# Request cross-attention in a decoder step: 32-column score groups, and values with the probabilities as stationary operand

## The reference, cut to what matters

```
def _cross_attn(h, mk, mv, w_cq, w_co):
    b, s, _ = h.shape
    q = (h @ w_cq).reshape(b, s, MEM_HEADS, MEM_HEAD_DIM)
    sc = jnp.einsum('bshd,bmhd->bhsm', q, mk).astype(jnp.float32) * (MEM_HEAD_DIM ** -0.5)
    p = jax.nn.softmax(sc, axis=-1).astype(mv.dtype)
    o = jnp.einsum('bhsm,bmhd->bshd', p, mv).reshape(b, s, MEM_WIDTH)
    return o @ w_co
```

## Time and profile before

| | |
|---|---|
| median of three runs | 2350.18 us |
| the profiled execution | 2351.52 us |
| its span in the trace | 2349.7 us |
| TensorE busy with products | 2241.3 us, 95% |
| VectorE busy | 1185.6 us, 50% |
| ScalarE busy | 300.5 us, 13% |
| moved by DMA | 843.21 MB, mean 359 GB/s |
| the changed stage, scores of v = 4 to the start of the output projection | 846.4 to 912.2 us |

### The profile page before, as it was taken

The page is one execution under the profiler, slowest core; times in us unless marked ns, Lnnn a source line. Parts: engine busy times, 40 slices in busy tenths (PEclk is TensorE's granted clock), DMA queues, the critical chain, the costliest instruction groups (busy, mean ns, idle before and its releaser), DMA issues.

```text
span 2349.7 us, 35545 instructions
## 1 busy us (share of the span) xinstructions
PE 2241.3 (95%) x14334; PEld 2050.4 (87%) x14334; DVE 1185.6 (50%) x2106; ACT 300.5 (13%) x923; POOL 370.0 (16%) x414
## 2 busy tenths in 40 slices
PE   7999998788889899999999999999999999999996
PEld 5677776576589889999999999999999999999996
DVE  3100004834376734867777644288644444444445
ACT  2000002612130001111111110144100000000001
POOL 0100000013201111222222221012211111111110
PEclk9999999999999988999999999999999999999998
DMA  7999962289859995899999999788999999999996
GB/s 290 399 410 390 395 259 80 105 345 372 327 202 403 373 346 216 338 395 421 422 421 421 418 422 420 289 307 339 367 422 422 422 422 422 422 422 421 421 422 247
DMA packets 117787, 843.21 MB, mean 359 GB/s; under 512 B 14432, under 2 KB 16608, under 8 KB 30656
## 3 DMA queue, kind: packets, MB, share of 16 engines
q1 hardware_dynamic: 62752, 485.30, 51.5%
q0 software_dynamic: 54128, 354.58, 37.3%
q10 hardware_dynamic: 816, 2.11, 0.2%
HBM read 834.25 MB, written 74.78 MB: 387 GB/s over the span
## 4 chain that ended last, share of the span: by engine, by line
PE 64%; DMA 26%; DVE 7%; ACT 1%; issue 1%; SPq 0%; POOL 0%; DVEq 0%; POOLq 0%; ACTq 0%
PE low L1383 50%; DMA BIG<-expert_v,VB 23%; PE big L1383 13%; DVE XT L1227 3%; DMA WR<-wall 1%; ACT BIG L607 1%; DMA BIG<-kaT 1%; DMA BIG<-memT 0%; DVE CST L939 0%; DVE BIG L816 0%; PE low L1513 0%; PE low L1559 0%; PE big L1733 0%; DVE CST L998 0%; DVE XT L1378 0%
## 5 line engine op out<-in xcount | busy, mean ns | idle before, releaser
L1383 PE MATMUL low<-HT,WR 128*128 128x176 f32 (+3 forms) x6336 | 1085.4, 334 | 7.3 <-DMA WR<-wall 6.0
L1383 PEld LDWEIGHTS low<-HT,WR 128*128 128x128 f32 x6336 | 989.8, 192 | 95.4 <-issue 7.7
L1227 DVE SCALAR_TENSOR_TENSOR XT<-BIG,VB,XT 128x2048 f32<-128x2048 f32 x128 | 301.0, 2352 | 333.5 <-DMA BIG<-expert_v,VB 333.2
L1383 PE MATMUL big<-BIG,WR 128*128 (+3 forms) x2888 | 451.0, 312 | 14.9 <-DVE XT L862 7.1
L1383 PEld LDWEIGHTS big<-BIG,WR 128*128 128x128 f32 x2888 | 417.6, 193 | 36.7 <-issue 24.6
L1383 PE MATMUL low<-BIG,WR 128*128 (+3 forms) x2616 | 434.5, 321 | 10.5 <-DMA WR<-wall 10.5
L1383 PEld LDWEIGHTS low<-BIG,WR 128*128 128x128 f32 x2616 | 411.5, 192 | 15.0 <-issue 10.6
L1214 DVE SCALAR_TENSOR_TENSOR BIG<-BIG 128x2048 f32<-128x2048 f32 x144 | 329.7, 2291 | 177.4 <-DMA BIG<-expert_u,VB 176.1
L519 POOL DMA_INDIRECT BIG<-expert_u,VB x144 | 164.2, 1140 | 763.1 <-DVE BIG L1214 683.5
L525 POOL DMA_INDIRECT BIG<-expert_v,VB x144 | 142.8, 991 | 591.8 <-DVE XT L1227 497.2
L885 DVE TENSOR_SCALAR BIG<-low 128x320 f32 x32 | 15.8, 492 | 264.0 <-PE low L1383 264.0
(11 more groups left out here) (226 smaller groups left out, 1107.4 us busy)
## 6 DMA issues: line engine op xcount, KB each, us to landing
WR<-uT SPq DMA_DIRECT2D x128, 1024.0 KB, 10.1
WR<-expert_v SPq DMA_DIRECT2D x128, 1024.0 KB, 14.5
WR<-wall SPq DMA_DIRECT2D x122, 1024.0 KB, 8.9
BIG<-va POOLq DMA_DIRECT2D x48, 512.0 KB, 8.7
BIG<-kaT POOLq DMA_DIRECT2D x64, 384.0 KB, 12.5
BIG<-kmT SPq DMA_DIRECT2D x2, 2048.0 KB, 10.2
BIG<-vm SPq DMA_DIRECT2D x8, 512.0 KB, 11.7
XT<-xT SPq DMA_DIRECT2D x1, 2560.0 KB, 21.6
```

Source lines behind the costliest of these rows:

```text
L1227: nc.vector.scalar_tensor_tensor(out=x_tok, in0=rows_of(row), scalar=weight, in1=x_tok, op0=ALU.mult, op1=ALU.add).then_inc(s_vsum, 1)
L1383: return nc.tensor.matmul(out, lhsT, rhs, start=start, stop=stop, skip_group_check=True)
```

## The change

The scores of a request group become 16 products with 32 columns each. The query block is laid out by request, and each head of it sits at its own 8 of 32 columns (`qpad_c` shrinks from 2176 to 512 words); request n writes only partitions 32n to 32n+32 of the bank, and the four heads add up there. The order is heads outside, requests inside, so that four products in a row use four different column groups. In the values, the probabilities of a request, transposed, are the stationary operand (32 columns), and all 512 value columns (4 heads x 128) the moving one: 8 products for a group, again four column groups in a row. That gives each row the values of all four heads. ScalarE copies the bank to `o_req`, and four more products with `own_head` (the identity with the rows of the other heads set to zero) turn it and pick each row's own head. VectorE prepares `is_head` and `own_head` ahead. The second request group moves from v = 9 to v = 8, and the last prompt head from v = 8 to v = 9. VectorE reorders group 0 in step 4 of the pipeline and group 1 at its end. The second group's values are now loaded when the four-column values of the first are done (`s_cV`), at the same place of the queue.

```
+        qpad_c = BIG[:, 11264:11776].rearrange("p (n h c) -> p n h c", n=4, h=4)
+        own_head = BIG[:, 11776:12288].rearrange("p (h c) -> p h c", h=4)
+        o_req = BIG[:, 12288:12800]
+        V_FIRST, V_REQ, V_ALL = 0, (4, 8), 10
+        HEAD_OF = {0: 0, 1: 1, 2: 2, 3: 3, 5: 0, 6: 1, 7: 2, 9: 3}
+        KEPT = {v: i + 1 for i, v in enumerate((0, 1, 2, 3, 5, 4, 6, 7, 9, 8))}
...
                 if before == POS["pq", 0, 12]:
-                    sp.wait_ge(s_cO, V_REQ[0] + 1)
+                    sp.wait_ge(s_cV, 1)
                     mem_values(1)
...  (ScalarE, in step it)
+                if 4 + it - 2 in V_REQ:
+                    r = V_REQ.index(4 + it - 2)
+                    act.wait_ge(s_cV, r + 1)
+                    nc.scalar.activation(o_req, bank[5], ACT.Copy).then_inc(s_cVev, 1)
...  (VectorE)
-            def out_requests():
-                dve.wait_ge(s_cO, V_ALL)
-                for r in range(2):
+            def out_requests(r):
+                dve.wait_ge(s_cO, KEPT[V_REQ[r]])
...
-                    nc.vector.memset(qpad_c, 0.0)
+                    nc.vector.memset(BIG[:, 11264:11776], 0.0)
+                    for h in range(4):
+                        nc.vector.tensor_scalar(own_head[:, h, :], ident, is_head[:, h:h + 1], None, ALU.mult)
...
-                if 4 <= it <= 7:
+                if 4 <= it <= 6:
                     out_c(v - 3)
+                if it == 4:
+                    out_requests(0)
                 if it < 7:
                     next_row()
-            out_requests()
+            out_c(9)
+            out_requests(1)
...  (TensorE, scores)
-                    for m in range(16):
-                        ins = mm(o, qpad_c[:, m * P:(m + 1) * P], km[:, m * MEM:(m + 1) * MEM], start=(m == 0), stop=(m == 15))
+                    for h in range(4):
+                        for n in range(4):
+                            ins = mm(o[32 * n:32 * n + 32, :], qpad_c[:, n, h, :], km[:, (4 * n + h) * MEM:(4 * n + h + 1) * MEM], start=(h == 0), stop=(h == 3))
...  (TensorE, values)
-                    for n in range(4):
-                        for h in range(4):
-                            m = 4 * n + h
-                            for b in range(2):
-                                ins = mm(bank[5][:, r * P + m * 8:r * P + m * 8 + 8], vm[n][:, b * 512 + h * P:][:, 0:P], pT[:, b * P + m * 8:b * P + m * 8 + 8], start=(b == 0), stop=(b == 1))
+                    if r:
+                        pe.wait_ge(s_cOev, KEPT[V_REQ[0]])
+                    for b in range(2):
+                        for n in range(4):
+                            ins = mm(bank[5][32 * n:32 * n + 32, :], pT[:, b * P + 32 * n:b * P + 32 * n + 32], vm[n][:, b * 512:(b + 1) * 512], start=(b == 0), stop=(b == 1))
+                    ins.then_inc(s_cV, 1)
...
+            def own_values_c(r):
+
+                pe.wait_ge(s_cVev, r + 1)
+                for h in range(4):
+                    ins = mm(bank[5][:, 0:P], o_req[:, h * P:(h + 1) * P], own_head[:, h, :], start=(h == 0), stop=(h == 3))
                 ins.then_inc(s_cO, 1)
...  (TensorE, in step it, behind the values)
+                if 4 + it - 3 in V_REQ:
+                    own_values_c(V_REQ.index(4 + it - 3))
```

More of the change, by code:

```diff
@@ L233, in build @@
         probsT_c = [BIG[:, at:at + 512].rearrange("p (b c) -> p b c", b=2) for at in (16000, 10240)]
-        qpad_c = BIG[:, 11264:13440]
+        qpad_c = BIG[:, 11264:11776].rearrange("p (n h c) -> p n h c", n=4, h=4)
+        own_head = BIG[:, 11776:12288].rearrange("p (h c) -> p h c", h=4)
+        o_req = BIG[:, 12288:12800]
+        is_head = stat[:, 76:80]
         km = BIG[:, 0:4096]
@@ L340, in build @@
         s_cpad = sem("c_pads")
+        s_cV, s_cVev = sem("c_request_values"), sem("c_request_values_kept")
         s_xt, s_ht = sem("tile0_turned"), sem("tile0_rows")
@@ L641, in turned_c @@
                 act.wait_ge(s_cT, v + 1)
-                if v >= 2:
-                    act.wait_ge(s_cO, v - 1)
+                if v - 2 in V_REQ:
+                    act.wait_ge(s_cV, V_REQ.index(v - 2) + 1)
+                elif v >= 2:
+                    act.wait_ge(s_cO, KEPT[v - 2])
                 nc.scalar.activation(probsT_of(v), turn_out(v), ACT.Copy).then_inc(s_cTev, 1)
@@ L1049, in pads_c @@
                 for h in range(4):
-                    dst = qpad_c.rearrange("p (n h c) -> p n h c", n=4, h=4)[:, :, h, 0:QPR]
+                    dst = qpad_c[:, :, h, QPR * h:QPR * (h + 1)]
                     src = qc[1][:, h, P + 32 * r:P + 32 * r + 32].rearrange("p (n q) -> p n q", q=QPR)
@@ L1068, in out_c @@
             def out_c(v):
-                dve.wait_ge(s_cO, v + 1)
-                dst = oc[0][:, v, :] if v < V_REQ[0] else oc[1][:, v - V_REST, 0:P]
+                dve.wait_ge(s_cO, KEPT[v])
+                dst = oc[0][:, v, :] if v < V_REQ[0] else oc[1][:, HEAD_OF[v], 0:P]
                 nc.vector.tensor_copy(dst, values_out(v)).then_inc(s_cOev, 1)
-            def out_requests():
-                dve.wait_ge(s_cO, V_ALL)
-                for r in range(2):
-                    for h in range(4):
-                        src = bank[5][:, r * P:(r + 1) * P].rearrange("p (n h q) -> p n h q", n=4, h=4)[:, :, h, :]
-                        dst = oc[1][:, h, P + 32 * r:P + 32 * r + 32].rearrange("p (n q) -> p n q", q=QPR)
-                        ins = nc.vector.tensor_copy(dst, src)
-                    ins.then_inc(s_cOev, 1)
+            def out_requests(r):
+                dve.wait_ge(s_cO, KEPT[V_REQ[r]])
+                for h in range(4):
+                    src = bank[5][:, 0:P].rearrange("p (n h q) -> p n h q", n=4, h=4)[:, :, h, :]
+                    dst = oc[1][:, h, P + 32 * r:P + 32 * r + 32].rearrange("p (n q) -> p n q", q=QPR)
+                    ins = nc.vector.tensor_copy(dst, src)
+                ins.then_inc(s_cOev, 1)
+            nc.vector.tensor_copy(is_head, head_mask.rearrange("p (h e) -> p h e", h=4)[:, :, 0])
             softmax_s(0)
@@ L1635, in scores_c @@
                 if V_FIRST + 2 <= v < V_REQ[0]:
-                    pe.wait_ge(s_cOev, v - 1)
+                    pe.wait_ge(s_cOev, KEPT[v - 2])
                 elif v >= V_REQ[0] + 2:
@@ L1643, in scores_c @@
                     pe.wait_ge(s_cpad, 4 * r + 4)
-                    for m in range(16):
-                        ins = mm(o, qpad_c[:, m * P:(m + 1) * P], km[:, m * MEM:(m + 1) * MEM], start=(m == 0), stop=(m == 15))
+                    for h in range(4):
+                        for n in range(4):
+                            ins = mm(o[32 * n:32 * n + 32, :], qpad_c[:, n, h, :], km[:, (4 * n + h) * MEM:(4 * n + h + 1) * MEM], start=(h == 0), stop=(h == 3))
                     ins.then_inc(s_cS, 1)
                 else:
-                    q = qc[0][:, v, :] if v < V_REQ[0] else qc[1][:, v - V_REST, 0:P]
-                    h = v if v < V_REQ[0] else v - V_REST
+                    h = HEAD_OF[v]
+                    q = qc[0][:, h, :] if v < V_REQ[0] else qc[1][:, h, 0:P]
                     mm(o, q, km_p[:, h * MEM:(h + 1) * MEM]).then_inc(s_cS, 1)
@@ L1665, in values_c @@
                     pe.wait_ge(s_vm[r], 4 * 16)
-                    for n in range(4):
-                        for h in range(4):
-                            m = 4 * n + h
-                            for b in range(2):
-                                ins = mm(bank[5][:, r * P + m * 8:r * P + m * 8 + 8], vm[n][:, b * 512 + h * P:][:, 0:P], pT[:, b * P + m * 8:b * P + m * 8 + 8], start=(b == 0), stop=(b == 1))
-                else:
-                    if v >= V_REST + 2:
-                        pe.wait_ge(s_cOev, v - 2)
-                    h = v if v < V_REQ[0] else v - V_REST
+                    if r:
[4 more added lines that the diff above has]
+                    ins.then_inc(s_cV, 1)
+                else:
+                    if v in (7, 9):
+                        pe.wait_ge(s_cOev, KEPT[5 if v == 7 else 7])
+                    h = HEAD_OF[v]
                     for b in range(2):
                         ins = mm(values_out(v), vm_p[:, b * 512 + h * P:b * 512 + (h + 1) * P], pT[:, b * P:(b + 1) * P], start=(b == 0), stop=(b == 1))
+                    ins.then_inc(s_cO, 1)
+            def own_values_c(r):
+                pe.wait_ge(s_cVev, r + 1)
+                for h in range(4):
+                    ins = mm(bank[5][:, 0:P], o_req[:, h * P:(h + 1) * P], own_head[:, h, :], start=(h == 0), stop=(h == 3))
                 ins.then_inc(s_cO, 1)
```

1 line of the change is left out of this document (removed).

## The result

| | before | after |
|---|---|---|
| median (four runs each, same chips) | 2349.59 us | **2325.97 us** |
| lowest to highest | 2346.76 to 2351.24 | 2323.5 to 2330.9 |
| profiled execution, its span | 2351.52, 2349.7 | 2326.72, 2324.9 |
| scores of v = 4 to start of the output projection | 65.8 us | 45.8 us |

The ratio after to before is 0.9907 with a 95% interval of 0.9892 to 0.9922: the kernel is about 0.9% faster. The forecast was 2324.2 us.

What follows compares the result with a forecast made beforehand. TensorE was taken to bound the changed stage, with DMA room: 32.1 us of work + 1.8 + 4.9 + 2.7 + 2.7 = 44.2 against 70.15 us, 26 us less, so 2324.2 us from median 2350.2; range 2316 to 2335.

Steps and rivals of the forecast that it cites:

- Scores in column groups: Request scores in the changed stage: 32 records at 58 ns, 1.85 us per group, 3.7 us for both.
- lost clock: At the stage's first scores, behind 3.10 us of TensorE idle time: 1.8 us lost, expected to stay.
- Values of the first group: Request values in the changed stage: 16 records of 512 moving columns, 1.85 us per group.
- Half clock at the end: Values of v = 8, picking and the four products behind run half at 1.2 GHz: 2.7 us more.
- Waits: TensorE's waits in the changed stage: 4.9 us for VectorE's steps plus 2.7 us for the second group's values.
- the late load: Second group's values before v = 8: landing at 880 us, wanted at 877.3, 2.7 us beyond 1.5 us already counted.
- Column groups that don't run side by side: Rival, 2%: no parallel column groups in the stage's scores and values, 20.6 us less gain, 2341 us.
- The DMA queue in TensorE's place: Rival, 9%: late values and gathers in the stage make TensorE wait; gain 10 to 16 us, 2334 to 2340 us.
- the wait for `vm`: Sign at the second group's values: the forecast is wrong if TensorE's wait for their load exceeds 5 us.
- the slower case: Rival, 3%: clock stays at 1.2 GHz behind the sparse steps into the output projection and beyond; up to 2360 us.
- given back: Rival, 3%: the stage's transfers pile up before the full DMA engines from 1036 us on; the end stays at 2350.
- Edits at nothing: Small edits counted as free: memset 1.87 to some 0.4 us, four scalings of 0.28 us, ScalarE's copy of 0.60 us.

Runs made afterwards that it cites:

- the change again: The changed kernel itself, unaltered, run on another chip beside later runs; median 2325.47 us, ratio 0.9898 to the kernel before.
- values loaded first: Changed kernel with the second group's values loaded ahead of the output projection's first two weight chunks; median 2318.53 us, ratio 0.9876 to the kernel before.
- values alone: Changed kernel with the request scores computed as before the change, values and picking kept; median 2329.56 us, ratio 0.9926 to the kernel before.
- other order: Changed kernel with the loop over requests outside, so products in a row use the same column group; median 2325.24 us, ratio 0.9901 to the kernel before.
- five rows later: Changed kernel with values loaded before two weight chunks, first query block laid out earlier, five expert rows moved out of the pipeline; 2317.29 us, 0.9864 to before.

## Why the prediction was right, point by point

**The bound.** Right: what TensorE lost in this stage came out at the end. From the start of the output projection to the end of the span it is 1437.5 us before and 1433.8 after; of the 3.7 us, 1.8 are the half clock in the first records of the earlier trace rows, now gone, and 1.7 a wait of TensorE for VectorE in the last stages, 7.4 us instead of 9.1. Nine further traces of changed kernels have 1434.0 to 1434.7 us here, whatever their stage gained; the change again has 1436.7, and only the two that move most rows out of the stage have more. Over the 70.15 us counted in the prediction the kernel now takes 48.44 us, 21.7 less; the stage began 1.2 us earlier (0.6 of it is there at 690 us already, 0.6 arises at a wait for a DMA near 760 us), and with the 1.7 us behind it these are 24.6 of the 24.8 us of the spans.

**Luck.** The stage gave 21.7 us and not the 26 forecast. Another 2.9 us (1.2 ahead of it, 1.7 behind) are from places that the change hardly touches and that differ from execution to execution: the stage starts between 842.98 and 847.81 us in traces whose instructions ahead of it are nearly the same, and the last wait is 5.6 us in the change again. That the total came within 2 us of the forecast is in part chance.

**The sum.** 48.44 us against 44.2 forecast. By terms, from start to start in the rows:
- Scores in column groups: 1.87 us for the second group, 1.85 forecast; the ideal, 8 x 0.221, is 1.77 us, so the two changes of mode around it cost 0.1 us at most. The first took 2.61 of the 3.65 forecast, and the tile behind it 4.54 instead of 3.58: 1.7 of the 1.8 us of lost clock were there, more than half of it one row later.
- Values of the first group 1.94 us, picking 0.90 at full clock: as forecast.
- Half clock at the end: 3.6 us lost (values of v = 8 1.7, picking 0.8, key products 0.4, small pieces 0.7), 2.7 forecast. The place was right, the size too small. The reason given, short pieces and a wait, is left open: with the load in time the clock was still at 0.50 in two kernels (values loaded first, values alone), nearly so in a third (other order, 0.56), and at 1.00 in a fourth (five rows later).
- The small products of the other units and the transpositions took 5.9 us at full clock, not 5.0: pieces of two or four records cost more than their count by the rate of long series.
- Waits: 9.9 us (0.31, 1.67, 7.43 and 0.47), 4.9 + 2.7 = 7.6 forecast.

**The mis-sized term** is the late load. The prediction put it at 880 us and the products' own demand at 877.3, with 1.5 us of wait ahead that it counted with VectorE's steps. It landed at 882.24 us, and the products were ready for it at 875.85 us. What they waited for until then was no step of VectorE but ScalarE's copy, 0.95 us; VectorE's scaling of v = 9, done at 877.8 us, is needed only behind them. So 4.2 us of wait were in the sum for this place, from 875.8 to 880 us, and 7.43 came, from 874.90 to 882.33 us: 2.3 us more because the load was later, 0.9 us more because TensorE was there earlier. The upper bound of 20.6 us after issue that the prediction took from the earlier trace rows belongs to the first group's loads at 800 us; the second group's landed 4.6 to 7.1 us after issue in the kernel before and up to 21.8 us after it here.

**The rivals.** Column groups that don't run side by side: refuted by 1.93 us for 32 records, 60 ns each, under the 100 ns that were the test. The DMA queue in TensorE's place was given 9% as a case of late gathers and a gain of 10 to 16 us. As a price it did not come: no gather held a step up. As a mechanism it is what happened: the DMA share is 1.02 for thirty microseconds, and the wait for `vm`, 6.4 of the 7.43 us, is over the 5 us that the prediction named as a sign of being wrong. By that sign one part of its account failed: DMA, not TensorE, sets the end of the stage now. The total came out near the forecast since 4.2 us of wait were in the sum for this place. The clock came back with the output projection, as it had before, so the slower case stayed away; nothing was given back at 1010 us.

**Edits at nothing.** The memset takes 0.48 us and the four scalings 0.74, and VectorE waits 4.94 us for a gather behind them, which takes both. The copy to `o_req` for the first group takes 0.59 us from 859.79 us, done 3.4 us before TensorE takes it up at 863.76. The Trainium skill (TensorEngine Tiling (Array Packing), PSUM Bottleneck) warns of such a copy behind a fourfold speed-up; in the changed stage the longest wait of TensorE for a copy of ScalarE was 0.95 us, and it was for the transposed probabilities; for `o_req` it never waited.

## What to carry to other kernels

When a stage bound by one engine is made a third shorter, ask first how many bytes have to arrive in it, and in which order: here the products came down by the forecast amount, but 2 MB of weights not yet needed stood ahead of the 2 MB that were, and moving them behind made the stage some 8 us shorter and the kernel some 7 us faster. Time that one edit saves may fall into a wait that another has opened, so halves of a change must be timed together before their gains are added. Work moved out of a crowded stage comes due in the next one, and past the point where that one waits for it, it brings nothing. And when a view gives a time from issue to landing, look which loads of the line it counted: here it had only those of another stage.

## What the runs showed of the hardware

- Products in different 32-column groups of TensorE need not alternate record by record: 32 records took 1.93 us taking turns one product (two records) at a time, 1.97 us with four records of one group in a row, 4.59 us with eight, and 7.07 us with 128 columns each. The gain of four groups was 7.07 / 1.93 = 3.7. The Trainium skill (TensorE: Matmul & The Clock Gate, Part 3) gives 2.38 for three groups with 512 moving columns; that case was not run here.
- 16 records with 512 moving columns took 1.92 us at granted clock 1.00, and 3.56 to 3.64 us at 0.50 (3.36 us in two kernels, where the stretch has 0.55 and 0.56). The low clock came behind waits of 7.43 and of 4.93 us and also behind 1.68 and 0.95 us with little work between them; with 2.14 us and with 0.78 us it stayed at 1.00, and behind 2.67 and 2.95 us the same records took 2.59 and 2.42 us, in part at either level. What decides between these cases the runs do not settle.
- The products with 8 moving columns lowered the clock to 0.50 with TensorE 100% busy, in both kernels that have them, and in none of the others did the query tile behind the first values take more than 3.74 us.
- With the DMA engines full (share 0.97 to 1.01 between issue and landing), taking two chunks of 1 MB out of the way of four loads of 0.5 MB changed their landing from 12.9 to 22.3 us after issue (the change again) to 6.2 to 12.1 us (values loaded first).
